# The order of the three products of a block pair in a two-block transformer kernel on one core

## What is computed

```python
def swiglu(x, w_gu, w_down):                     # first block, both layers
    gate, up = jnp.split(x @ w_gu, 2, axis=-1)
    return (jax.nn.silu(gate) * up) @ w_down
...
def swiglu_ffn(x, w_in, w_out):                  # second block, twice a layer
    a, b = jnp.split(x @ w_in, 2, axis=-1)
    return (jax.nn.silu(a) * b) @ w_out
...
    (qa, ckv, iq, ik, iw, qs, ks, vs, cb, cc, ch, ga, gb, gc) = jnp.split(x @ w_in, offsets, axis=-1)
    merged = (jax.nn.sigmoid(ga + b_gate[0]) * (y_a @ w_branch[0])
              + jax.nn.sigmoid(gb + b_gate[1]) * (y_b @ w_branch[1])
              + jax.nn.sigmoid(gc + b_gate[2]) * (y_c @ w_branch[2]))
    return merged @ w_out
```

## Time and profile before

| | |
|---|---|
| median of 3 runs | 2230.66 us (2228.38 to 2231.65) |
| the profiled execution | 2233.17 us, of which the span is 2231.4 us |
| mean granted TensorE clock | 0.995 |
| PE busy | 2203.0 us (99%), 16007 matmuls |
| PEld busy | 2047.8 us (92%), 16007 loads |
| DVE, ACT, POOL busy | 1435.2, 1074.0, 118.4 us |
| chain that ended last | PE 91%, DVE 5%, DMA 1%, ACT 1% |
| read from HBM | 406.44 MB, 184 GB/s over the span |

### The profile page before, as it was taken

One profiled execution on the slowest core, in us unless ns is written; L12 is line 12 of the kernel. 1 busy time (PEld: TensorE's weight loads), 2 busy tenths in 40 slices (PEclk: granted clock), 3 DMA queues, 4 the chain that ended last, 5 costly groups with the idle time before them and its releaser, 6 DMA issues.

```text
span 2231.4 us, 38216 instructions
## 1 busy us (share of the span) xinstructions
PE 2203.0 (99%) x16007; PEld 2047.8 (92%) x16007; DVE 1435.2 (64%) x1678; ACT 1074.0 (48%) x1320; POOL 118.4 (5%) x206
## 2 busy tenths in 40 slices
PE   9999999999999999999999999999999999999998
PEld 8989899888989989998999998998998999998997
DVE  6885655577655555556876676556556876677555
ACT  4554444357454443443556464443443555555442
POOL 2300000020000000000011000000000002000000
PEclk9999999999999999999999999999999999999999
DMA  8756555674645665566454655565565554564553
GB/s 245 217 180 207 170 184 191 191 210 143 207 151 184 195 226 170 189 218 199 151 157 143 201 196 180 190 217 180 190 203 190 181 168 154 158 233 158 189 180 122
DMA packets 349595, 413.92 MB, mean 185 GB/s; under 512 B 12013, under 2 KB 281513, under 8 KB 349297
## 3 DMA queue, kind: packets, MB, share of 16 engines
q1 hardware_dynamic: 339232, 377.19, 52.8%
q0 software_dynamic: 10192, 34.29, 5.0%
HBM read 406.44 MB, written 5.00 MB: 184 GB/s over the span
## 4 chain that ended last, share of the span: by engine, by line
PE 91%; DVE 5%; DMA 1%; ACT 1%; issue 1%; SPq 0%; POOL 0%; DVEq 0%; ACTq 0%
PE bank L360 91%; DMA raw<-in_even_w_in 1%; DVE wl L1850 0%; DVE x L1964 0%; DVE qkT L2133 0%; DVE z L1959 0%; DVE stat L1925 0%; DVE front_l L1850 0%; ACT wh L1291 0%; DVE z L1923 0%; DMA lamt<-in_odd_lambda 0%; DVE em_l L1850 0%; ACT em_h L1291 0%; DVE qkT L2131 0%; SPq L2749 0%
## 5 line engine op out<-in xcount | busy, mean ns | idle before, releaser
L1850 DVE TENSOR_TENSOR wl<-raw,wh 128x2048 fp32r<-128x2048 f32 (+2 forms) x344 | 759.0, 2212 | 506.5 <-ACT wh L1291 423.7
L360 PE MATMUL bank<-xl,wh 128*128 128x256 f32 x3144 | 877.4, 279 | 6.0 <-issue 5.2
L360 PE MATMUL bank<-xh,wl 128*128 128x256 f32 x3144 | 871.1, 277 | 0.0
L360 PE MATMUL bank<-xh,wh 128*128 128x256 f32 x3144 | 870.9, 277 | 0.0
L1291 ACT ACTIVATE wh<-raw 128x2048 fp32r<-128x2048 f32 (+2 forms) x344 | 634.9, 1850 | 317.3 <-PE bank L360 299.1
L360 PEld LDWEIGHTS bank<-xl,wh 128*128 128x128 f32 x3144 | 591.5, 188 | 13.3 <-issue 11.2
L360 PEld LDWEIGHTS bank<-xh,wl 128*128 128x128 f32 x3144 | 591.5, 188 | 0.6
L360 PEld LDWEIGHTS bank<-xh,wh 128*128 128x128 f32 x3144 | 591.3, 188 | 0.2
L360 PE MATMUL bank<-wl,hh 128*128 128x512 f32 x528 | 205.9, 390 | 0.0
L360 PE MATMUL bank<-wh,hh 128*128 128x512 f32 x528 | 205.5, 389 | 0.0
L360 PE MATMUL bank<-wh,hl 128*128 128x512 f32 x528 | 205.4, 389 | 0.0
(11 more groups left out here) (395 smaller groups left out, 3157.6 us busy)
## 6 DMA issues: line engine op xcount, KB each, us to landing
raw<-in_ffn_w_in SPq DMA_DIRECT2D x80, 1024.0 KB, 5.2
raw<-in_w_mix_in SPq DMA_DIRECT2D x56, 1024.0 KB, 5.3
raw<-in_ffn_w_gu SPq DMA_DIRECT2D x40, 1024.0 KB, 5.2
raw<-in_ffn_w_out SPq DMA_DIRECT2D x40, 1024.0 KB, 5.1
raw<-in_ffn_w_down SPq DMA_DIRECT2D x20, 1024.0 KB, 5.1
raw<-in_mem_wkv SPq DMA_DIRECT2D x16, 1024.0 KB, 5.4
raw<-in_even_w_in SPq DMA_DIRECT2D x12, 1024.0 KB, 6.5
raw<-in_w_branch SPq DMA_DIRECT2D x24, 512.0 KB, 3.6
```

The lines of the kernel that those rows point to most:

```text
L360: ins = pe.transpose(o, a, b) if transpose else pe.matmul(o, a, b, start=start, stop=stop)
L1850: dve.tensor_tensor(part_of(t, 1)[:, half:], raw_tile(t)[:, half:], part_of(t, 0)[:, half:].bitcast(F32), ALU.subtract).then_inc(sig("w_lo ...
```

## The change

`three` issues the product with the low stationary part first and the product with the low moving part second. The third is as before.

```diff
         def three(o, ah, al, bh, bl, first, last, full=None):
-            mm(o, ah, bl, first, False)
-            mm(o, al, bh, False, False)
+            mm(o, al, bh, first, False)
+            mm(o, ah, bl, False, False)
             mm(o, ah, bh, False, last, full)
```

## The result

The changed kernel takes 2243.1 us (median of six runs, 2240.4 to 2247.8) where the kernel before, beside it, takes 2230.1 us (2228.4 to 2231.7). The ratio is 1.0061, 95% interval 1.0048 to 1.0074: **slower by 0.6%**, 13 us. The profiled execution took 2240.6 us, with a span of 2238.8.

A forecast was written before the change was run, and what follows sets the result against it. The prediction took PE's matmul spacing to bound the kernel (PE busy 2203.0 of 2231.4 us). Its four parts, 0 us each, left the median at 2230.7 us, with a range of 2219 to 2250 us.

The forecast's parts named there:

- What bounds the kernel: PE, busy 2203.0 of 2231.4 us: kernel time is close to the number of matmuls times their spacing.
- Part 1, waits: PE's waits and the other engines' queues: the same semaphores are awaited, nothing starts earlier or later, 0 us.
- Part 2, the moving stream: Each PE product streams the same columns, so a triple takes 340 ns in either order: 0 us.
- Part 3, the repeated weights: PE's third product repeats the second's stationary operand; its load is done again in full: 0 us.
- The estimate of 13 us less: PE, if one load in three fell away: some 4 ns less for each of 3,300 triples, 13 us.
- Part 4, the pairs that overlap: On PE, new pairings of streaming product and next weight load: between -16 and +12 (or +37) us, taken as 0.
- Rival A: Short PE stretches outside the FFNs: 2,600 products slower by 4.6 ns each, 12 us, 2243 us; chance 0.28.
- If the FFNs go too, it is 2267 us: Worse case of Rival A: the FFNs' products on PE turn slow as well, 2267 us.
- Rival B: Slow PE stretches lose part of their excess: half of 16 us gives 2223 us, all 2215 us; chance 0.22.
- What would show it: Signs on PE: 16007 loads at 188 to 192 ns, about 797 FFN matmuls in 90 us, m by w about 172.

The follow-up runs named there:

- the changed kernel with old entries: Changed kernel, but the block_products matmuls (including the 144 ahead of each FFN's long run) keep the order of before: 2229.7 us, ratio to before 1.0002.
- the one with transposes: Changed kernel plus six identity transposes between the block_products matmuls and the long run of each FFN: 2234.2 us, ratio to before 1.0020.

## Why the prediction was right or wrong

**What bounds the kernel: right.** PE is 92% of the chain, and every microsecond lost is one of matmul spacing.

**Part 1, waits: right.** The largest wait is 7.2 us (before 7.1), and no other engine or queue moved.

**Part 2, the moving stream: right at the fast pace.** 113.3 ns in the new order, in half of the long runs of after and in all six of the changed kernel with old entries. 512 columns: (50 + 0.39) / 223 = 226 ns.

**Part 3, the repeated weights: right.** PEld has 16,007 loads as before. These are the loads of the changed kernel in its first long run (slow), then one of its fourth (fast):

```profile
L360 PEld LDWEIGHTS bank<-xh,wl 128*128 128x128 f32 x255 | 49.0, 192 | 0.0
L360 PEld LDWEIGHTS bank<-xl,wh 128*128 128x128 f32 x256 | 48.1, 188 | 0.0
L360 PEld LDWEIGHTS bank<-xh,wh 128*128 128x128 f32 x255 | 47.9, 188 | 0.0
...
L360 PEld LDWEIGHTS bank<-xh,wl 128*128 128x128 f32 x265 | 49.8, 188 | 0.0
```

The load of the operand that is already there (that for `xh,wh`) takes 188 ns like any other. The estimate of 13 us less, worked out from "load once and matmul repeatedly" (the Trainium skill, page "TensorE: Matmul & The Clock Gate", section "Step-by-step: what each phase is for"), has no counterpart in this trace. At the slow pace one load of three is recorded at 192 ns, as in the earlier trace rows, only it is now the load for the first product instead of the third.

**Part 4, the pairs that overlap: here it failed.** I bounded it at -16 to +12 us, took 0, and it was 3 x 3.8 = 11.5 us. The number is inside the bound, by luck, since it came from the place that the bound had left out. The step that failed is "5,472 stand in the long runs of the six FFNs ... So I hold them for the firmest". The rows showed that a run keeps its pace for 90 us. I read that as firmness of the run. What they show is that a run does not leave a pace once it has one, and that is just as true of the slow pace. The question was what happens at its first products, which is one moment in each FFN, and there before had come from slow to fast six times of six; the new entry stays slow three times of six in the profile shown. The rows of that moment were in the trace (the 0.13 us ahead) and I did not look at them. The count was a little off too: the unbroken run is 18 tiles, and the nineteenth stands behind transposes of z, where it was slow once in the kernel before.

The reason that I gave for 0, that the stream sets the spacing and has 3 ns of room beside the load, is true of the fast pace and says nothing on which of the two paces is taken.

**Rival A was the right mechanism at the wrong place.** It priced 2,600 products outside the FFNs at 12 us, 2243 us in all, and the median is 2243.1; that the two agree is luck. For outside the FFNs the change is near zero (y by w 276, 277 and 279 ns where 276, 276 and 278 stood; m by w slow as before). Its sentence "If the FFNs go too, it is 2267 us" took all of them or none, and in the profile it was half. Rival B, faster, did not happen anywhere: m by w stayed at the slow pace.

**What would show it** worked: the count in 90 us of an FFN (797, or 765 if A at its worst) named the fault at first sight, three rows with 766 and 767. The window of m by w I expected at 172; at 162:182 it has 169, because the stretch ends at 181.2 us in this execution. One microsecond earlier it has the 172:

```profile
161.00:181.00 20.00, 20.00 (x172) 20.00 (x171) 15.48 (x13) 9.21 (x8) 1.10 (x2) 1.00 0.88 291
```

The median lies 13.0 us above before, a little more than the three runs of the profile are worth. The runs of after differ by up to 7.4 us among themselves, twice the 3.3 of before. The clock doesn't explain it: three of them at the same mean granted clock, 0.996, took 2240.6, 2246.3 and 2247.8 us. 3.8 us more or less for each long run would do it. Only profiled runs show their long runs, so how many are slow in the others wasn't measured.

**What stays open.** What inside PE chooses the pace, and why the slow one costs 4.4 ns. Whether the repeated stationary operand or only the departure from the old order matters. Which part of the entry's order matters, and whether the entries of the other sublayers, turned along with those of the FFNs, have a share in it. Why the last three FFNs mostly stay fast in the changed kernel (of the variants of the order, the fifth was slow in two, and the fourth in the one with transposes).

## What to carry to other kernels

A chain of back-to-back matmuls, each with a weight load of its own, can have two steady paces, and here it kept the one it started with until something broke the chain. (Loads follow each other at 110 ns here and the fast pace is 113; that this closeness is the reason was not shown.) So judge a change of order or of place by what stands just ahead of each long run, and there by its first few starts in the timeline; the order of the 144 products ahead bore on 864 behind them. Look for the pace as a count of matmuls in a window of fixed length, for each long run apart: the mean duration of a group moved by 2 ns, while the windows differed by 30 matmuls.

## What the runs showed of the hardware that was not expected

- Two steady spacings at one clock (1.00, the 2.4 GHz level) for the same instructions on the same tiles: 113.3 and 117.7 ns for 256 columns, 4% apart, each held over 90 us.
- The pace depends on what ran before: with only the entries' order changed the runs behind them went from FFFFFF to SSFFFF, and six transposes in between dealt them anew.
- The place of the moving operand matters at 64 bytes: `x` moved by 64 gave 118.6 ns in all six long runs and 2.1% on the whole kernel; `m` moved by 64 gave 118.6 for 117.9.
- The places of the operands ahead matter as well: with those of the entries moved, and `x` and `w` left where they were, all six long runs were slow.
